# Self-attention of a decoder layer: VectorE combines the last step before it takes the two maxima of this one, and the ratio's second factor is a column scalar

## The reference, cut to what matters

```python
def block(i):
    start = i * Q_BLOCK                                    # 8 blocks of 128 queries
    qb = lax.dynamic_slice_in_dim(q, start, Q_BLOCK, axis=3)
    s = jnp.einsum('bhcqd,bhckd->bhcqk', qb, k) * scale    # 4 heads h, two score maps c
    causal = (start + jnp.arange(Q_BLOCK))[:, None] >= key_pos[None, :]
    s = jnp.where(causal, s, -jnp.inf)
    p = jax.nn.softmax(s, axis=-1)
    attn = p[:, :, 0] - lam * p[:, :, 1]
    return jnp.einsum('bhqk,bhkv->bhqv', attn, v)
```

## Time and profile before

| | us |
|---|---|
| median of 3 runs | 1472.22 (1471.67 to 1473.21) |
| the profiled execution | 1470.95 |
| its span | 1469.2 |
| busy in the span: PE | 1437.9 (98%) |
| busy: PEld | 1200.0 (82%) |
| busy: DVE | 926.7 (63%) |
| busy: ACT | 679.6 (46%) |
| granted TensorE clock over the span | 0.998 |

### The profile page before, as it was taken

One profiled execution on the slowest core, in us unless ns is written; L12 is line 12 of the kernel. 1 busy time (PEld: TensorE's weight loads), 2 busy tenths in 40 slices (PEclk: granted clock), 3 DMA queues, 4 the chain that ended last, 5 costly groups with the idle time before them and its releaser, 6 DMA issues.

```text
span 1469.2 us, 20027 instructions
## 1 busy us (share of the span) xinstructions
PE 1437.9 (98%) x7440; PEld 1200.0 (82%) x7440; DVE 926.7 (63%) x1498; ACT 679.6 (46%) x1377; POOL 86.8 (6%) x132
## 2 busy tenths in 40 slices
PE   9999999998989999999999999999999999999998
PEld 7889888885669988888988777888888788888886
DVE  4873565638885424423622798887776585467898
ACT  6324222328885424424622666444444464444443
POOL 1000000000010001000000360000000000000012
PEclk9999999999999999999999999999999999999999
DMA  8212010102003610110021333654343697765463
GB/s 318 60 30 58 29 31 28 58 2 85 1 1 127 246 57 3 58 58 29 1 72 58 129 123 115 222 199 175 143 151 129 235 343 260 260 226 188 157 229 129
DMA packets 92304, 177.16 MB, mean 121 GB/s; under 512 B 9904, under 2 KB 28336, under 8 KB 90160
## 3 DMA queue, kind: packets, MB, share of 16 engines
q1 hardware_dynamic: 87312, 153.30, 30.8%
q10 hardware_dynamic: 4896, 22.58, 4.7%
HBM read 138.10 MB, written 37.75 MB: 120 GB/s over the span
## 4 chain that ended last, share of the span: by engine, by line
PE 86%; DVE 5%; ACT 4%; issue 3%; DMA 1%; SPq 1%; POOL 1%; ACTq 0%; DVEq 0%; POOLq 0%
PE ps L2094 25%; PE ps L2096 25%; PE ps L2095 25%; PE ps L2412 2%; PE ps L2150 1%; ACT probs L999 1%; DVE nmax L1620 1%; PE ps L2233 1%; DMA x_in<-in_x_dram 1%; PE ps L2292 1%; PE ps L2330 1%; DVE wq_l L1847 1%; PE ps L2311 1%; PE ps L2236 1%; ACT junk L839 0%
## 5 line engine op out<-in xcount | busy, mean ns | idle before, releaser
L2094 PE MATMUL ps<-wh,oph 128*128 128x512 f32 (+1 forms) x576 | 216.1, 375 | 0.0
L2096 PE MATMUL ps<-wh,opl 128*128 128x512 f32 (+1 forms) x576 | 212.0, 368 | 0.0
L2095 PE MATMUL ps<-wl,oph 128*128 128x512 f32 (+1 forms) x576 | 212.0, 368 | 0.0
L2094 PE MATMUL ps<-d_ring 128*128 128x512 f32 x448 | 175.1, 391 | 2.1 <-DVE d_ring L1968 2.1
L2096 PE MATMUL ps<-d_ring 128*128 128x512 f32 x448 | 175.1, 391 | 0.0
L2095 PE MATMUL ps<-d_ring 128*128 128x512 f32 x448 | 175.0, 391 | 0.0
L766 POOL TENSOR_TENSOR rms<-stat,mhalf 128x1 f32<-128x1 f32 (+2 forms) x59 | 50.5, 859 | 1332.5 <-DVE stat L1351 1311.2
L2096 PEld LDWEIGHTS ps<-wh,opl 128*128 128x128 f32 x576 | 108.3, 188 | 19.3
L2095 PEld LDWEIGHTS ps<-wl,oph 128*128 128x128 f32 x576 | 108.4, 188 | 17.9
L2094 PEld LDWEIGHTS ps<-wh,oph 128*128 128x128 f32 x576 | 108.3, 188 | 17.9 <-ACT vt L959 0.2
L1269 ACT ACTIVATE d_ring<-left_raw 128x512 fp32r<-128x512 f32 x112 | 70.3, 627 | 98.7 <-PE ps L2096 77.1
(11 more groups left out here) (354 smaller groups left out, 2928.3 us busy)
## 6 DMA issues: line engine op xcount, KB each, us to landing
right_raw<-in_w_down_dram SPq DMA_DIRECT2D x128, 256.0 KB, 3.8
u_kept_s<-us SPq DMA_DIRECT2D x64, 256.0 KB, 2.7
left_raw<-u_kept_s SPq DMA_DIRECT2D x64, 256.0 KB, 2.9
w_blk<-in_w_up_blocks_dram ACTq DMA_DIRECT2D x14, 1024.0 KB, 5.7
left_raw<-u_kept_a SPq DMA_DIRECT2D x48, 256.0 KB, 3.0
raw<-in_w_in_dram SPq DMA_DIRECT2D x16, 512.0 KB, 3.9
u_kept_a<-u SPq DMA_DIRECT2D x24, 256.0 KB, 2.2
x_in<-in_x_dram SPq DMA_DIRECT2D x8, 512.0 KB, 9.1
```

Source lines behind the costliest of these rows:

```text
L2094: te.matmul(o, lh, rh, start=first, stop=False)
L2095: te.matmul(o, lh, rl, start=False, stop=False)
L2096: return te.matmul(o, ll, rh, start=False, stop=last)
```

## The change

In VectorE's loop the combination of step n - 1 comes first in iteration n, and both maxima of step n follow it. The ratio's instruction becomes a TENSOR_SCALAR on one column, whose two factors are both columns of one value for each partition (`recs` and `lam`), where it was a SCALAR_TENSOR_TENSOR that read one of them as a scalar and the other as its second stream.

```diff
-                after(v.scalar_tensor_tensor(ratio[:, n % 2:n % 2 + 1], sums[:, n % 4, 0:1], recs[:, n % 4, 1:2],
-                                             lam[:, 4:5], ALU.mult, ALU.mult))
+                after(v.tensor_scalar(ratio[:, n % 2:n % 2 + 1], sums[:, n % 4, 0:1], recs[:, n % 4, 1:2], lam[:, 4:5],
+                                      ALU.mult, ALU.mult))
...
             for n in range(NS + 7):
-                if n < NS:
-                    attn_max(n, 0)
                 if 1 <= n <= NS:
                     attn_comb(n - 1)
                 if n < NS:
+                    attn_max(n, 0)
                     attn_max(n, 1)
                 if n < 3:
                     y_norm(5 + n)
```

## The result

The changed kernel takes 1487.7 us (median of 4 runs, 1487.12 to 1488.58) against 1472.72 us before (4 runs, 1471.67 to 1473.3): a ratio of 1.0103, with a 95% interval of 1.009 to 1.0115. It is 15 us slower, where 14.7 were forecast (1487.0 us). The profiled execution took 1488.02 us, with a span of 1486.3.

The account below looks back on a forecast made before the run. TensorE, busy 91.50 of the stage's 100.64 us, was taken to yield the pace to a VectorE-ScalarE loop: stretches summing to 115.30 us, +14.66 on 1470.95 as profiled, 1485.6, plus 1.27 for the median, giving 1487 us (1480.5 to 1491).

Parts of the forecast that it names:

- The loop: VectorE and ScalarE: exponential 1, combination, maximum 0, longer of maximum 1 and exponential 0, exponential 1; one more maximum per step, +14.66 us.
- The links: Handover and instruction times between exponential, reciprocal, combination and maxima, read from rows; errors allowed at 0.09 us in each of 31 steps.
- The four stretches: Reciprocals 0 to 7, 7 to 15, 15 to 23, 23 to 31: forecast 30.67, 33.07, 27.70, 23.86 us; sum 115.30 against 100.64.
- step 8: Step into 896 keys: 4.51 us, with ScalarE's other work, 2.52 us at worst, hidden under a 2.54 us wait.
- The normalisation of the memory tokens: VectorE at 384 keys: 2.39 us of work into a gap of 0.97, so it costs 1.42 us.
- The ratio: VectorE's new ratio instruction takes 280 ns against 219, adding 0.06 us in each of 31 steps, 1.9 us inside the sum.
- The clock: the rival: TensorE idles more and its clock falls from 2.4 to 1.2 GHz: +25 us or more; chance 0.04.
- What the profile should show: Exponentials' waits for maxima rise from 10.4 to about 30 us or more; TensorE busy 91.5 us at clock 1.00; pair 8.9 us.
- faster: Earlier combination lets TensorE's transposes start sooner, removing their 4.6 us of waits: 1466.4 us as profiled; chance 0.02.
- no change: Stage is TensorE's from end to end, or the loop has slack enough, so the time stays; chance 0.03.

Follow-up runs that it names:

- experiment 2: Kernel before with only the new ratio instruction (TENSOR_SCALAR), in the old order: 1473.73 us, ratio to before 1.0006.
- 4: Changed kernel with each maximum taken over the first 128 keys only, not the whole row: 1475.67 us, ratio to before 1.0021.
- 5: Kernel before (old order, old ratio) with each maximum taken over the first 128 keys only: 1468.55 us, ratio to before 0.9974.
- 6: Kernel before with the new order in long steps (even n) only, old ratio instruction: 1477.49 us, ratio to before 1.0036.
- Experiment 1: Changed kernel with the old ratio instruction (SCALAR_TENSOR_TENSOR) put back, so the new order alone: 1486.23 us, ratio to before 1.0093.
- experiment 7: Kernel before with both maxima ahead of the combination in short steps (odd n) only, old ratio instruction: 1471.16 us, ratio to before 0.999.
- 8: Kernel before with both maxima ahead of the combination in odd steps and in all steps from n = 24 on: 1470.93 us, ratio to before 0.9989.
- experiment 3: Kernel before with both maxima of step n ahead of the combination of n-1 in every step: 1475.86 us, ratio to before 1.002.

## Why the prediction was right, and where it was not

**The loop: right, and shown.** One more maximum lies between exponential 1 of one step and exponential 1 of the next. Three kinds of edit agree with that: take the order back (experiment 2), shorten the maxima (4 against 5), put one into every second loop (6, within 0.1 us of the sum). Experiment 1 shows that it is the order and not the ratio: with the old ratio nearly the whole loss stays.

**The links: right.** The four stretches came out at -0.20, +0.69, -0.11 and -0.10 us from the forecast. That the sum is only 0.28 us off is in part luck: step 8 is 0.85 us longer than forecast (next point), and the other thirty together 0.57 shorter, some 0.02 each.

**Step 8, mis-sized.** The prediction took ScalarE's other work ahead of a long step as 2.52 us at worst, hidden under a wait of 2.54. In the step into 896 keys it was not hidden: 4.51 us forecast, 5.36 measured. ScalarE's squares of the memory tokens (`m_junk`) stand between exponential 1 of step 7 and exponential 0 of step 8, together with the evacuations of a long step:

```profile
369.55 1.05 ACT L839 ACTIVATE m_junk<-m_in 128x1024 f32<-128x1024 f32 x1
...
372.45 0.60 ACT L1016 ACTIVATE probs_t<-ps 128x512 f32<-128x512 f32 x1 [0.66 <-PE ps L2310]
372.94 1.00 ACT L999 ACTIVATE probs<-ps,nmax 128x896 f32<-128x896 f32 x1
```

Exponential 0 starts right behind the second evacuation and waits for no maximum. At full clock this way takes 4.91 us (experiment 1), 0.40 more than the loop was forecast to take. The step takes 4.90 or 4.91 us in the profiles of the kernel before and of the experiments 1, 2, 4, 5, 6, 7 and 8, whatever their order, ratio and length of maxima, so none of these sets its pace. The other 0.45 us are the spell of half clock in the profiled execution: the second evacuation waited 0.66 us for TensorE's transposes, and 0.20 in experiment 1. The normalisation of the memory tokens, which was in the sum, made step 9 4.90 us long (3.50 + 1.42 = 4.92 forecast).

**The ratio: right in sign and size.** 273 ns in the changed kernel, where 280 were taken from rows of wider instructions. The rule of the Trainium skill, page "VectorE: DVE Perf Modes", section "The TRN2 errata", by which both forms cost the same, would have given 1.9 us less; the measured 273 against 219 ns decide against it here.

**The clock: the rival occurred in a small form.** I wrote that every new gap of TensorE would be shorter than 2 us and that the clock would stay at 1.00. Neither held. The clock was at its lower level, 1.2 GHz, for parts of the first two stretches (0.94 and 0.95 above). Ahead of these spells TensorE had idled 1.82 and 2.15 us:

```profile
343.79 1.03 PE L2310 MATMUL ps<-ident,probs 128*128 128x128 f32 x4 [1.82 <-ACT probs_t L1016]
...
371.33 1.09 PE L2310 MATMUL ps<-ident,probs 128*128 128x128 f32 x4 [2.15 <-ACT probs_t L1016]
```

At full clock four such transposes take 0.63 us: so they do in experiment 1, at the place of the second row, behind a gap of 2.11 us. So a gap within the bound of 2 us that the prediction trusted was followed by a spell too, and the earlier trace rows, one stretch of the kernel before, could not exclude it. The longer matrix products are most of the reason why TensorE's busy time is 95.08 us and not 91.50: in experiment 1, with a granted clock of 0.99 to 1.00 in all four stretches, it is 92.27. The first spell cost nothing: step 2, in which most of it lies, is 4.87 us long, step 4 without it 4.85. The second made step 8 0.45 us longer, as said above.

A third spell lies in the stages behind and was paid for. Both kernels reach the same transposes 400.04 us after reciprocal 31, behind the same wait for VectorE. After (start, us, instruction, idle before):

```profile
854.90 1.09 PE L2435 MATMUL ps<-ident,h_tok 128*128 128x128 f32 x8 [2.11 <-DVE h_tok L1785]
...
856.21 0.63 PE L2094 MATMUL ps<-opl,wq_h 128*128 128x512 f32 x1
```

Before:

```profile
839.52 1.09 PE L2436 MATMUL ps<-ident,h_tok 128*128 128x128 f32 x8 [2.10 <-DVE h_tok L1786]
...
840.69 0.40 PE L2095 MATMUL ps<-opl,wq_h 128*128 128x512 f32 x1
```

ScalarE's first copy of the down projection's weights into its ring (L1269) starts 710.6 us after reciprocal 31 before (1150.1) and 712.2 after (1167.1): 1.6 of the 1.72 us. That is one execution of each. It is not a steady price of the change: the profile of experiment 1, also in the new order, has no such spell at this place, that of experiment 3 has one. The medians, 15.0 us apart, fit the 14.94 us of distance without it.

**What the profile should show: one number wrong.** The waits of exponentials for maxima were to rise from 10.4 to 30 us or more:

```profile
ACT probs L999 <- DVE nmax L1620: 22.1, 26, 2.5
DVE recs L1629 <- ACT probs L999: 18.5, 20, 1.3
```

They rose to 22.1. A part of the time in which ScalarE could not go on is booked elsewhere: it waited for TensorE with its outputs (2.8 us, 1.3 before) and evacuations (3.3 us, 2.3 before). That it would have waited for the maximum in this time anyway is argued and not shown, and the rest of the gap to 30 stays open. The rivals "faster" and "no change" did not occur: TensorE's waits for combinations stayed (4.6 before, 4.5 after), where the prediction had thought that they may vanish, and the pair left 7.40 us.

## What to carry to other kernels

Where two engines hand tiles to each other in a loop, find the loop and add up what stands in it, link by link, with each in-order queue's position counted; busy shares don't show it, for here VectorE is busy 84% of the distance before and 75% after the loss. Add the other way into each step as well: in step 8 it was the longer one. An instruction that can run early should stand ahead of the one that waits, as long as what it needs itself is there in time (experiment 7). Experiment 3 shows the other side: early maxima whose scores are not ready delay the combination that a third engine waits for.

## What the runs showed of the hardware

- A column scalar has a price of its own on VectorE. TENSOR_SCALAR takes 160 ns on 128x4 with constants, 229 with one column scalar there, 272 or 273 on 128x1 with two. SCALAR_TENSOR_TENSOR takes 159 ns on 128x1 with a constant (L2068 of the kernel before) and 219 with one column scalar. Here, where one factor can be read as the second stream, that form is the shorter one.
- A gap of 2.1 us on TensorE can be followed by half clock or not. The same gap, 2.10 and 2.11 us long ahead of the same transposes, was followed by matmuls of 0.40 us in one profile and 0.63 in the other. A gap of 1.82 us was followed by half clock too. Over 29 runs of the kernel before, the fastest (1470.70 us) had a mean clock of 0.998 and the slowest (1476.22) one of 0.996. By an estimate from these numbers the clock accounts for some 0.002 * 1470 = 2.9 us, about half of the spread of 5.5 us.
